# One edit of a mixture-of-experts decoder kernel: put-backs, the norm row's spread and the spatial weights moved, and the last two output slots of a mixer used token tile by token tile

## The chip, the cores and the metric

The kernel runs on one core of a Trainium2 chip. The metric is the device time of one execution in microseconds (us); the median of several executions counts. The engines are TensorE (PE in the rows; its weight loads are PEld), VectorE (DVE), ScalarE (ACT), GpSimd (POOL) and SyncE (SP), whose queue issues most DMAs.

## What is computed

Four layers on 256 tokens of width 1024, all in float32. Mixers: layers 0 and 3 a short gated convolution, layer 1 retention, layer 2 a gated MLP with spatial weights `c_w_s`.

```python
for i in range(DEPTH):                                  # 4
    mix = (conv, retention, sgu)[i % 3](x)
    x = layer_norm(ALPHA * x + mix, ln_g[i, 0], ln_b[i, 0])
    ffn = moe(x)              # 16 experts, 4 groups, top 2, router shared by the layers
    x = layer_norm(ALPHA * x + ffn, ln_g[i, 1], ln_b[i, 1])
    emb = p[i] @ ple_w_proj[i]
    x = x + sigmoid(x @ ple_w_gate[i] + ple_b_gate[i]) * emb
```

## The kernel before

**Tiling.** The tokens are two tiles (t = 0, 1) of 128. `x` holds the current rows. Each engine has one hand-written program, and they meet in semaphores. PSUM banks 0 to 3 are the sums of tile 0 (columns 0 to 511, 512 to 1023) and tile 1; banks 4 to 7 are for transposes and the rest.

**Weights.** Dense weights come in *slots* of 1 MB, loaded by SyncE into the six places of `raw`. ACT copies a slot rounded into `w_hi`, DVE makes the rest `w_lo` = `raw` - `w_hi` (`split_slot`, L1556 in the rows). A product is three matmuls (L637, L638, L639: high by high, low by high, high by low). A slot takes 12 matmuls for each tile; I call that a slot-half. `weights_used` counts slots that tile 1 has finished with; loads into their place and splits two or three slots later wait for it. Experts' weights, 96 slots a layer (8 pairs of experts, 12 slots each), are used as they are, in matmuls 64 columns wide (L1033). They are spread over all places that are free at the time: `raw`, `w_hi`, `work`, even `x` (the last one). SyncE issues all loads in one written order, each behind a wait for its place, so a load that waits holds up those behind it.

**A layer.** `first_group` and the further groups of `project_slot` are the mixer's input product; `first_group` also transposes tile 1 of `x`, the embedding `p_in` (`turn_p`) and, in layer 2, the spatial weights. Then comes the output product in rows (`rows_slot`), `last_rows` for its last three slots. The last slot of each tile ends with column half 0 and then half 1 (`half_done`, `mix_done`), and DVE starts to add it to `x` by halves (`add_rows`, L1599, with statistics L1600) and then makes the layer norm of the tile (`layer_norm`, last step L1654), tile 0 first and then tile 1. TensorE transposes tile 0 (`transpose_tile`, L648), computes part of the embedding product (L982) and the router's logits (L975), runs two filler matmuls, transposes tile 1, and finishes the logits. ACT and DVE choose the experts (`route`); TensorE computes each token's rank (L1003 to L1007), and DVE the table `pick` (`choose`, four calls).

**Experts.** For each pair p TensorE gathers (L1025), does gate and up (`wide`), transposes (`turn`), does `down`, and `put` adds the outcome y of pair p - 2 to the tiles' sums (`put_back`, L1043). For pairs 3 to 6 (`LATER`) only tile 0 is put back at once, tile 1 in the end (`put_later`). `add_x` (L1081) adds the old `x`. Behind the last `down`, the put-backs of pair 7 complete tile 0's halves (`put_half`, `ffn_done`) and then tile 1. DVE takes statistics (L1604) and makes the second layer norm. TensorE runs filler matmuls (`keep_running`, L654), transposes tile 0 and starts the gate product: `gate_slot`, whose first two slots of tile 0 are whole float32 matmuls (L788), while the next need `w_lo`. During tile 1's part DVE already builds the next layer's `x`.

**GpSimd** fetches the small rows and broadcasts them over the partitions (`load_norm` into `ln_par`, `c_ln`, `bgate`). For the next layer's first norm it waits for `x_tile_ready` = 6L + 4, when the second norm of this layer is done.

## Time and profile before

| | us |
|---|---|
| three runs | 1614.87, 1614.98, 1615.57 |
| median | 1614.98 |
| the profiled execution | 1615.02 |
| its span (first to last instruction) | 1613.2 |
| TensorE busy in the span | 1600.2 |
| DVE, ACT, GpSimd busy | 689.4, 460.4, 46.5 |
| mean granted clock of TensorE | 0.999 |
| HBM | 330 GB/s over the span; 420 to 423 in the experts |

Times in rows are us from the span's start. "Idle before" in brackets is the engine's idle time ahead of a row's first instruction and what ended it. The row of a weight load (PEld) is the best place to see TensorE wait, since matmuls' ends are modelled; some idle of 0.2 to 0.3 us ahead of a wide load is the usual pace.

### The profile page before, as it was taken

The page shows a single profiled execution, that of the slowest core. Times are in us where ns is not written, and L with a number is a line of the kernel's source. Part 1 is how long each engine was busy: PE and PEld are TensorE (multiplying, and loading weights), DVE is VectorE, ACT ScalarE, POOL GpSimd, SP SyncE. Part 2 cuts the span into 40 slices and gives each one's busy share as a digit, 9 for nine tenths or more (in the row PEclk, how much of TensorE's full clock was granted, in tenths as well). Part 3 has the DMA queues.
Part 4 walks back from the last instruction along what each step waited for, and adds up shares of the span by engine and source line. Part 5 has one row for each costly group of instructions (what it writes and reads, how often), then busy time and mean ns, then how long its engine had stood idle before and what let it go on. Part 6 is the DMA issues. An engine that isn't in the chain of part 4 may idle for free.

```text
span 1613.2 us, 17962 instructions
## 1 busy us (share of the span) xinstructions
PE 1600.2 (99%) x7576; PEld 961.3 (60%) x7584; DVE 689.4 (43%) x1023; ACT 460.4 (29%) x557; POOL 46.5 (3%) x47
## 2 busy tenths in 40 slices
PE   9999999999999999999999999999999999999998
PEld 7874433478877744433788888643434887444335
DVE  5671111294757711111956755511115767211117
ACT  5522111154433221111544433211102452211113
POOL 1000000010000000000110000000010000000000
PEclk9999999999999999999999999999999999999999
DMA  6989999946636799999557556999997388999992
GB/s 262 371 368 401 423 420 421 421 176 266 243 132 243 281 414 423 421 421 421 222 200 280 182 205 235 389 397 421 421 420 324 141 343 375 385 422 421 421 421 102
DMA packets 75146, 534.43 MB, mean 331 GB/s; under 512 B 8976, under 2 KB 9136, under 8 KB 10544
## 3 DMA queue, kind: packets, MB, share of 16 engines
q1 hardware_dynamic: 73728, 530.95, 81.2%
q0 software_dynamic: 1328, 2.21, 0.4%
q8 instruction: 65, 1.06, 0.3%
q14 instruction: 25, 0.20, 0.0%
HBM read 532.07 MB, written 1.05 MB: 330 GB/s over the span
## 4 chain that ended last, share of the span: by engine, by line
PE 90%; DVE 6%; DMA 3%; ACT 1%; issue 1%; SPq 0%; DVEq 0%; ACTq 0%
PE psum L1033 39%; PE psum L637 12%; PE psum L639 12%; PE psum L638 12%; PE psum L1025 4%; PE psum L648 3%; PE psum L1043 3%; DVE w_lo L1556 2%; PE psum L982 2%; DMA x<-in_experts 1%; DMA raw<-in_experts 1%; PE psum L975 1%; PE psum L927 1%; PE psum L872 1%; DVE x L1647 0%
## 5 line engine op out<-in xcount | busy, mean ns | idle before, releaser
L1556 DVE TENSOR_TENSOR w_lo<-raw,w_hi 128x2048 fp32r<-128x2048 f32 (+1 forms) x128 | 272.5, 2145 | 187.2 <-ACT w_hi L1248 186.7
L637 PE MATMUL psum<-w_hi,xT_hi 128*128 128x512 f32 x672 | 265.3, 395 | 3.0 <-DVE w_lo L1556 3.0
L1248 ACT ACTIVATE w_hi<-raw 128x2048 fp32r<-128x2048 f32 (+1 forms) x128 | 221.4, 1751 | 155.7 <-PE psum L639 113.1
L639 PE MATMUL psum<-w_hi,xT_lo 128*128 128x512 f32 x672 | 261.8, 390 | 0.0
L638 PE MATMUL psum<-w_lo,xT_hi 128*128 128x512 f32 x672 | 261.6, 389 | 0.0
L1248 ACT ACTIVATE work<-psum 128x512 f32<-128x512 f32 x152 | 85.8, 597 | 349.0 <-PE psum L648 247.3
L637 PEld LDWEIGHTS psum<-w_hi,xT_hi 128*128 128x128 f32 x672 | 126.2, 188 | 30.6 <-DVE w_lo L1556 4.5
L1033 PE MATMUL psum<-raw,xg 128*64 128x512 f32 x624 | 143.8, 594 | 0.0
L639 PEld LDWEIGHTS psum<-w_hi,xT_lo 128*128 128x128 f32 x672 | 126.1, 188 | 26.7
L638 PEld LDWEIGHTS psum<-w_lo,xT_hi 128*128 128x128 f32 x672 | 126.3, 188 | 25.8 <-issue 0.2
L1952 DVE TENSOR_REDUCE cg<-psum 128x1 f32<-128x256 f32 x32 | 13.6, 425 | 233.9 <-PE psum L1103 233.9
L1556 DVE TENSOR_TENSOR work_r<-psum,work_r 128x512 fp32r<-128x512 f32 x52 | 34.5, 688 | 183.7 <-ACT work_r L1248 183.7
L1248 ACT ACTIVATE xg<-psum 128x512 f32<-128x512 f32 x84 | 49.8, 597 | 203.3 <-PE psum L1025 102.1
L1033 PE MATMUL psum<-expert_work,xg 128*64 128x512 f32 x448 | 103.5, 594 | 0.0
L1033 PEld LDWEIGHTS psum<-raw,xg 128*64 128x64 f32 x624 | 43.9, 137 | 84.5 <-issue 83.9
L1033 PE MATMUL psum<-raw,work 128*64 128x512 f32 x400 | 92.9, 593 | 0.5 <-DMA raw<-in_experts 0.3
L637 PE MATMUL psum<-w_hi,work_r 128*128 128x512 f32 x224 | 89.2, 398 | 0.8 <-ACT work L1248 0.8
L639 PE MATMUL psum<-w_hi,work_r 128*128 128x512 f32 x224 | 87.6, 391 | 0.0
L638 PE MATMUL psum<-w_lo,work_r 128*128 128x512 f32 x224 | 87.5, 391 | 0.0
L1033 PE MATMUL psum<-expert_high,xg 128*64 128x512 f32 x336 | 79.5, 594 | 0.0
L1556 DVE TENSOR_TENSOR w_hi<-psum,w_hi 128x512 fp32r<-128x512 f32 x24 | 16.6, 692 | 141.7 <-ACT w_hi L1248 141.7
L1248 ACT ACTIVATE work_r<-psum 128x512 fp32r<-128x512 f32 x52 | 29.4, 600 | 159.7 <-PE psum L1033 156.2
(172 smaller groups left out, 1712.8 us busy)
## 6 DMA issues: line engine op xcount, KB each, us to landing
raw<-in_experts SPq DMA_DIRECT2D x128, 1024.0 KB, 15.9
raw<-in_slots SPq DMA_DIRECT2D x120, 1024.0 KB, 4.9
expert_work<-in_experts SPq DMA_DIRECT2D x88, 1024.0 KB, 15.4
expert_high<-in_experts SPq DMA_DIRECT2D x60, 1024.0 KB, 12.2
expert_spare<-in_experts SPq DMA_DIRECT2D x40, 1024.0 KB, 13.2
expert_bias<-in_experts SPq DMA_DIRECT2D x20, 1024.0 KB, 13.9
x<-in_experts SPq DMA_DIRECT2D x20, 1024.0 KB, 15.6
expert_norm<-in_experts SPq DMA_DIRECT2D x16, 1024.0 KB, 13.7
```

What stands on the lines that cost most here:

```text
L637: mm(out, lhs[0], rhs[0], start=start, stop=False)
L638: mm(out, lhs[0], rhs[1], start=False, stop=False)
L639: return mm(out, lhs[1], rhs[0], start=False, stop=stop)
L648: last = nc.tensor.transpose(psum[:, bank, i * P:(i + 1) * P], c, ident[:, :])
L872: last = mm(psum[:, 4 + k % 4, :], sT[:, h, (c + s) * P:(c + s + 1) * P], rv[:, s, h * DV:(h + 1) * DV], start=s == 0, stop=s == c)
L927: mm(tiles(psum[:, 4 + k % 4, 0:SVB]), sgu_wT[:, b // 2, :], sv[:, c, 3 * b:3 * b + 3, :], start=True, stop=True).then_inc(vs_in_psum, 1)
L982: last = mm(psum[:, 2 * t + c, :], pT[:, j, t * P:(t + 1) * P], whole[:, 2 * j + c, :], start=j == 0, stop=j == 1)
L1025: last = mm(psum[:, bank, j * SEQ:(j + 1) * SEQ], x_split[a][:, t, chunk], pick[:, t, Q * SEQ:(Q + 1) * SEQ], start=t + a == 0, stop=t + a ...
L1033: last = mm(psum[columns(e), bank, :], lhs(j, e), w[:, 2 * j + e, :], start=start and j == 0, stop=stop and j == 1)
L1043: last = mm(psum[:, bank0 + 2 * t + c, :], where[:, t * P:(t + 1) * P], what[i][:, c * NB:(c + 1) * NB], start=start and i == 0, stop=stop ...
L1248: return nc.scalar.activation(dst, src, func)
L1556: return tt(lo, whole, hi.bitcast(F), ALU.subtract)
```

## The change

Five things are moved; the arithmetic stays.

- GpSimd: the first `load_norm` of layers 1 to 3 is no longer made at the end of the layer before but in the layer itself, once its first six slots are used; `p_in` is fetched when the first column half of `x` is ready.
- Spatial weights (layer 2): their transposes go from before slot 3 of tile 0, bank 3, to behind `turn_p` in tile 1's part, bank 4; ACT's copy moves with them, and TensorE waits for it two slots into tile 1.
- The end of the mixer: of the last three slots the first is now used by both tiles in turn, and only the last two tile by tile.
- Put-backs: those of pair 6 for tile 0 stand behind the last `down` instead of before it; those of pair 4 for tile 1 stand with the others behind `add_x(1)`. Of the fillers, three ahead of tile 0's transposes and two behind them are dropped.
- `choose` for tile 0's first four experts stands ahead of the wait for the second rank.

```diff
--- before.py
+++ after.py
@@ -597,7 +597,7 @@
                     pool.wait_ge(x_tile_ready, 6 * L - 1)
                     pool.dma_start(sgu_w, A["c_w_s"][0].rearrange("g t s -> t g s")).then_inc(sw_loaded, 16)
                 if L:
-                    pool.wait_ge(x_tile_ready, 6 * L)
+                    pool.wait_ge(x_half_ready, 6 * L)
                     pool.dma_start(p_in, A["p"][L, 0].rearrange("(t p) d -> p t d", p=P)).then_inc(p_loaded, 16)
                 if L % 3 == 1:
                     pool.dma_start(rot, A["rotary"]).then_inc(b_loaded, 16)
@@ -607,15 +607,15 @@
                         pool.dma_start(c_ln[0:1, a, :], A[name][0].unsqueeze(0)).then_inc(gate_norm_row, 16)
                     pool.wait_ge(gate_norm_row, 32)
                     spread(c_ln[:, :, :].rearrange("p a n -> p (a n)"), c_loaded, 32)
+                if L:
+                    pool.wait_ge(weights_used, starts[L][0] + 6)
+                    load_norm(L, 0)
                 pool.wait_ge(experts_used, last_use(L, ("norm", 0)))
                 load_norm(L, 1)
                 pool.wait_ge(experts_used, last_use(L, ("bias", 0)))
                 pool.dma_start(bgate[0:1, :], A["ple_b_gate"][L].unsqueeze(0)).then_inc(bias_row, 16)
                 pool.wait_ge(bias_row, 16 * (L + 1))
                 spread(bgate[:, :], bg_loaded, 16)
-                if L + 1 < DEPTH:
-                    pool.wait_ge(x_tile_ready, 6 * L + 4)
-                    load_norm(L + 1, 0)
 
 
         @block.tensor
@@ -719,19 +719,19 @@
                 for i in range(4):
                     if i == 3:
                         transpose_tile(3 * L, 1)
-                        if L % 3 == 2:
-                            pe.wait_ge(sw_masked, 1)
-                            transpose4(3, [sgu_w[:, g, :] for g in range(SGROUPS)]).then_inc(sw_in_psum, 1)
                     project_slot(L, 0, 0, i)
                 turned_tile(3 * L, 1)
-                if L % 3 == 2:
-                    pe.wait_ge(sw_ready, 1)
                 for i in range(4):
                     if i == 2:
                         pe.wait_ge(pt_ready, L + 1)
+                        if L % 3 == 2:
+                            pe.wait_ge(sw_ready, 1)
                     project_slot(L, 0, 1, i)
                     if i == 0:
                         turn_p(L)
+                        if L % 3 == 2:
+                            pe.wait_ge(sw_masked, 1)
+                            transpose4(4, [sgu_w[:, g, :] for g in range(SGROUPS)]).then_inc(sw_in_psum, 1)
 
             def rows_slot(n, count, lhs, q, t, i, done):
 
@@ -762,8 +762,9 @@
 
             def last_rows(L, n, count, lhs):
 
+                rows_both(n, count, lhs, count - 3)
                 for t in range(T):
-                    for i in range(1, 4):
+                    for i in range(2, 4):
                         rows_slot(n, count, lhs, count // 4 - 1, t, i, mix_done)
                 transpose_tile(3 * L + 1, 0)
 
@@ -829,10 +830,10 @@
                     rows_slot(n, 4, tiled(gT), 0, t, 0, mix_done)
                     if t == 0:
                         turn_b(1)
+                rows_both(n, 4, tiled(gT), 1)
                 for t in range(T):
-                    for i in range(1, 4):
-                        if i == 2:
-                            pe.wait_ge(gT_ready[L], 3 + t)
+                    pe.wait_ge(gT_ready[L], 3 + t)
+                    for i in range(2, 4):
                         rows_slot(n, 4, tiled(gT), 0, t, i, mix_done)
                 transpose_tile(3 * L + 1, 0)
 
@@ -1156,19 +1157,17 @@
                 turn(PAIRS - 1)
                 pe.wait_ge(ident_ready, 1)
                 add_x(0)
-                put(PAIRS - 2)
                 pe.wait_ge(ht_ready, PAIRS * (L + 1))
                 down(PAIRS - 1, 0, 4)
                 pe.wait_ge(place_ready, PAIRS * (L + 1))
                 down(PAIRS - 1, 1, 7)
 
-                pe.wait_ge(y_ready, 2 * PAIRS * (L + 1) - 1)
-                put_back(place_of(PAIRS - 1), y, 0, 0, False, True).then_inc(put_half, 1)
-                put_later(LATER[1])
-                pe.wait_ge(y_ready, 2 * PAIRS * (L + 1))
-                put_back(place_of(PAIRS - 1), y, 0, 1, False, True).then_inc(ffn_done, 1)
+                for c in range(2):
+                    put_back(place_of(PAIRS - 2), outputs(L, PAIRS - 2), 0, c, False, False)
+                    pe.wait_ge(y_ready, 2 * PAIRS * (L + 1) - 1 + c)
+                    put_back(place_of(PAIRS - 1), y, 0, c, False, True).then_inc((put_half, ffn_done)[c], 1)
                 add_x(1)
-                for p in (LATER[0], *LATER[2:]):
+                for p in LATER:
                     put_later(p)
                 for c in range(2):
                     last = put_back(place_of(PAIRS - 1), y, 1, c, False, True)
@@ -1227,9 +1226,8 @@
                 experts(L)
 
                 pe.wait_ge(general_done, L + 1)
-                keep_running(3, 5)
                 transpose_tile(3 * L + 2, 0)
-                keep_running(3, 1)
+                keep_running(1, 1)
                 for i in range(4):
                     if i == 2:
                         transpose_tile(3 * L + 2, 1)
@@ -1289,6 +1287,9 @@
                     if (q, b, t) == (0, 0, 1):
                         act.wait_ge(pt_in_psum, L + 1)
                         copy(pT, psum[:, 3, :].rearrange("p (j n) -> p j n", j=2)).then_inc(pt_ready, 1)
+                        if L % 3 == 2:
+                            act.wait_ge(sw_in_psum, 1)
+                            copy(sgu_wT, quad(4)).then_inc(sw_ready, 1)
                     wait_block(act, L, b, t, proj_in_psum[L])
                     save(b, t, psum[:, 2 * t + b % 2, :]).then_inc(proj_ready[L], 1)
                     if t:
@@ -1299,9 +1300,6 @@
                 n = starts[L][0]
                 split_behind(n)
                 save_tile(3 * L, 1)
-                if L % 3 == 2:
-                    act.wait_ge(sw_in_psum, 1)
-                    copy(sgu_wT, quad(3)).then_inc(sw_ready, 1)
                 save_group(L, 0, save)
 
             def conv_mixer(L):
@@ -1900,11 +1898,12 @@
                 dve.wait_ge(rank_in_psum, 2 * L + 1)
                 link(stt(key[:, :, :], psum[:, 5, 0:T * NE].rearrange("p (t e) -> p t e", t=T), 1.0,
                          chosen[:, :, :], ALU.add, ALU.mult))
+                choose(0, slice(0, 4)).then_inc(pick_ready, 1)
                 dve.wait_ge(rank_in_psum, 2 * (L + 1))
                 step(ts(big[:, :], psum[:, 4, 0:NE], HALF + 0.5, None, ALU.is_gt))
-                for part in (slice(0, 4), slice(4, NE)):
-                    for t in range(T):
-                        choose(t, part).then_inc(pick_ready, 1)
+                choose(1, slice(0, 4)).then_inc(pick_ready, 1)
+                for t in range(T):
+                    choose(t, slice(4, NE)).then_inc(pick_ready, 1)
 
                 link(nc.vector.tensor_reduce(den[:, :], cw[:, :, :], X, ALU.add))
                 link(nc.vector.tensor_reduce(bigmax[:, :], big[:, :], X, ALU.max))
```

## Rows read from the trace of the kernel before

**Rows 1.** The page, busy us (share of the span) x instructions:
```profile
PE 1600.2 (99%) x7576; PEld 961.3 (60%) x7584; DVE 689.4 (43%) x1023; ACT 460.4 (29%) x557; POOL 46.5 (3%) x47
```
**Rows 2.** Timeline, DVE, mixer's end, layer 0: start, us, instruction [idle before]:
```profile
92.45 0.69 DVE L1599 SCALAR_TENSOR_TENSOR x<-x,psum 128x512 f32<-128x512 f32 x1 [2.70 <-PE psum L639]
...
98.41 1.42 DVE L1654 SCALAR_TENSOR_TENSOR x<-x,nrstd,ln_par 128x512 f32<-128x512 f32 x2
100.85 0.69 DVE L1599 SCALAR_TENSOR_TENSOR x<-x,psum 128x512 f32<-128x512 f32 x1 [1.03 <-PE psum L639]
```
**Rows 3.** Timeline, layer 1: DVE at tile 1, and TensorE's transposes of it:
```profile
549.25 0.69 DVE L1599 SCALAR_TENSOR_TENSOR x<-x,psum 128x512 f32<-128x512 f32 x1 [0.83 <-PE psum L639]
...
556.08 0.42 PEld L648 LDWEIGHTS psum<-const,x 128*128 128x128 f32 x4 [0.42 <-DVE x L1654]
556.74 0.42 PEld L648 LDWEIGHTS psum<-const,x 128*128 128x128 f32 x4 [0.24 <-DVE x L1654]
```
**Rows 4.** DMA share (last but one) at 149; landing: issues 149.16, 597.53, 1062.14, 1405.60:
```profile
149.00:150.00 1.00, 1.00 (x8) 0.39 (x6) 0.00 (x0) 0.85 (x2) 0.00 (x0) 1.00 0.06 25
...
DMA to landing us min/median/max: 5.2/5.2/5.2
...
DMA to landing us min/median/max: 6.0/6.0/6.0
...
DMA to landing us min/median/max: 4.7/4.7/4.7
...
DMA to landing us min/median/max: 5.5/5.5/5.5
```
**Rows 5.** Timeline, weight loads at the last expert slots, layers 0, 1, 2, 3:
```profile
314.50 0.14 PEld L1033 LDWEIGHTS psum<-x,work 128*64 128x64 f32 x2 [0.34 <-DMA x<-in_experts]
...
763.82 0.20 PEld L1033 LDWEIGHTS psum<-x,work 128*64 128x64 f32 x4 [0.94 <-DMA x<-in_experts]
...
1227.43 0.14 PEld L1033 LDWEIGHTS psum<-x,work 128*64 128x64 f32 x2 [0.29 <-DMA x<-in_experts]
...
1562.12 0.20 PEld L1033 LDWEIGHTS psum<-raw,work 128*64 128x64 f32 x4 [1.22 <-DMA raw<-in_experts]
...
1572.06 0.20 PEld L1033 LDWEIGHTS psum<-x,work 128*64 128x64 f32 x4 [0.92 <-DMA x<-in_experts]
```
**Rows 6.** Timeline, layer 0 ahead of the last `down`: TensorE, and ACT's `hT`:
```profile
308.55 0.76 PEld L1043 LDWEIGHTS psum<-xT_hi,work_r 128*128 128x128 f32 x4 [0.40 <-issue]
309.68 0.20 PEld L1033 LDWEIGHTS psum<-expert_high,work 128*64 128x64 f32 x4 [0.37 <-issue]
...
307.69 0.60 ACT L1248 ACTIVATE work<-psum 128x512 f32<-128x512 f32 x1
```
**Rows 7.** Timeline, layer 0, from the put-backs to the gate product:
```profile
322.23 0.87 PEld L1043 LDWEIGHTS psum<-work_r 128*128 128x128 f32 x4
...
323.81 1.01 PEld L648 LDWEIGHTS psum<-const,x 128*128 128x128 f32 x8
...
325.33 0.41 PEld L788 LDWEIGHTS psum<-raw,xg 128*128 128x128 f32 x2
...
324.13 1.29 DVE L1604 BATCH_NORM_STATS2 stats<-psum 128x6 f32<-128x512 f32 x2
```
**Rows 8.** Timeline, gate product, layer 0; the last row is layer 3's:
```profile
330.49 6.44 DVE L1556 TENSOR_TENSOR w_lo<-raw,w_hi 128x2048 fp32r<-128x2048 f32 x2
...
332.58 2.35 POOL L584 PARTITION_BROADCAST ln_par<-ln_par  x1 [1.33 <-DMA ln_par<-in_ln_b]
...
336.99 0.19 PEld L637 LDWEIGHTS psum<-w_hi,xT_hi 128*128 128x128 f32 x1 [1.21 <-DVE w_lo L1556]
...
1587.70 4.48 DVE L1556 TENSOR_TENSOR w_lo<-raw,w_hi 128x2048 fp32r<-128x2048 f32 x2
```
**Rows 9.** Timeline, start of layer 2, DVE and TensorE:
```profile
807.71 2.28 DVE L1556 TENSOR_TENSOR w_lo<-raw,w_hi 128x2048 fp32r<-128x2048 f32 x1
...
810.65 0.42 PEld L648 LDWEIGHTS psum<-const,emb 128*128 128x128 f32 x4 [1.06 <-DVE emb L1794]
811.04 0.19 PEld L637 LDWEIGHTS psum<-w_hi,xT_hi 128*128 128x128 f32 x1
```
**Rows 10.** Timeline, TensorE at the kernel's start:
```profile
0.99 3.59 PE L669 MATMUL psum<-ones 128*128 128x256 bf16 x16 [0.99 <-POOL ones L577]
...
6.12 2.35 PE L669 MATMUL psum<-ones 128*128 128x256 bf16 x20
```

## The prediction

> **What bounds the kernel now.** I read the busy table first: TensorE is busy for 99% of the span [rows 1]. The kernel holds some 7,500 matmuls and the change removes only eight filler matmuls (two in each of four layers). So time can move only where TensorE waits. I then went through its weight-load rows for gaps longer than the usual one, and through the chain that ended last. Each layer has four places where another resource decides.
> (a) *Between mixer and router.* The transposes of token tile 1 wait for DVE's layer norm: 0.42 and 0.24 us of idle in layer 1 [rows 3].
> (b) *Inside and at the end of the experts.* The last weight slot, which lands in `x`, is used the moment it arrives. In layers 0 and 2 TensorE is there at the same time. In layers 1 and 3 it waits: 0.94 and 0.92 us instead of the usual 0.29, and in layer 3 another 1.22 us a little earlier [rows 5].
> (c) *In the gate product.* DVE's split of a weight slot is late by 1.2 us, in layers 0, 1 and 2 but not in 3 [rows 8].
> (d) *At the start of layer 2.* TensorE waits 1.06 us for the mask of the spatial weights [rows 9].
>
> **Part 1, the row spread.** In layers 0 to 2 GpSimd fetches and broadcasts the next `ln_par` just when DVE makes the two `w_lo` that the gate product waits for. Two such subtractions take 6.44 us beside the 2.35 us broadcast, and 4.48 us in layer 3, where there is none [rows 8]. So the broadcast costs DVE 1.96 us and TensorE some 1.16 us of the 1.21 of idle (0.05 is usual between such loads). Moved to `weights_used` = first + 6, the broadcast falls into the projections. TensorE shows no wait for `w_lo` there, since slots are split two to three slots ahead of use (12 matmuls at 0.23 us for each token tile, 5.5 us a slot). I price its new place at 0. Without that cover it costs at most the same 1.96 us in each of layers 1 to 3. What is queued behind it on GpSimd (the second `load_norm`) waits for the experts anyway. The earlier fetch of `p_in` is worth 0: nobody waits for it.
>
> The Trainium skill (SBUF — State Buffer, Who interferes with whom) says that a DVE operation with two SBUF inputs contends with a GpSimd instruction that reads SBUF. By that rule the collision is moved, not removed, wherever a `w_lo` meets the broadcast again. The trace agrees on the collision; it cannot show the new one.
>
> **Part 2, put-backs and fillers.** The four put-back matmuls of pair 6 for tile 0 leave the place before `down(7)`. There they cost 309.68 - 308.55 = 1.13 us; with the fixed switch of some 0.4 us between kinds of matmul, and `hT` copied by 308.29, `down(7)` can start at 308.5, so 1.15 us earlier [rows 6]. That pays only where TensorE, not a DMA, is last (below). Behind `down(7)` the first six matmuls are as many as before, so `ffn_done` for tile 0 comes at the same distance. But four put-backs of pair 4 now stand behind it: 24 instead of 20 matmuls, 4 x 0.22 = 0.9 us more. Against that stand the removed fillers: three ahead of the transposes (0.45 us), which now start 0.46 us later, and two behind them, which lay beside ACT's copy. The first gate matmul at 325.33 waits for this copy [rows 7], so it comes 0.46 us later, too. The second tile's statistics, at 324.13 when DVE came free, wait for the later put-back: +0.37 us for DVE.
> Together with part 1: the gate product's late slot (336.99) could start at 336.99 - 1.16 + 0.46 = 336.29, and DVE has it by 336.93 - 1.96 + 0.37 = 335.34. TensorE is now last. Gain 1.16 - 0.46 = **0.70 us in each of layers 0 to 2, together -2.1**. In layer 3 there was no wait to win: **+0.46**.
>
> **Part 3, spatial weights.** Layer 2 loses the wait at 810.65. But `w_lo` for the same slot ends at 809.99 [rows 9], so slot 3 can start at 810.05 at the earliest instead of 811.04: 0.99. The four transposes (0.42 us and a switch) are paid later, behind `turn_p`, and 2.7 us of matmuls cover the ACT copy that is now waited for. **-0.5 us.**
>
> **Part 4, the choice of slots** (`choose` ahead of `big`) is the same work in another order, and TensorE has `embed` matmuls to do meanwhile: 0.
>
> **Part 5, the last output slots.** This is the largest term, and it is a loss. DVE starts on tile 0 at 92.45, when the first half is summed, and ends its norm at 98.41 + 1.42 = 99.83: 7.38 us. It then idles 1.03 us until tile 1's half comes at 100.85 [rows 2]. The two halves are three slot-halves apart (8.4 us). In the new order they are two apart, 5.6 us. So DVE comes to tile 1 late by 7.38 - 5.6 = 1.77 us in layer 0, and by 2.75 - 0.83 = 1.92 in layer 1 [rows 3]; layers 3 and 2 repeat these within 0.01. The transposes of tile 1 already wait for this norm, so the router and the first expert start **R = 1.77, 1.92, 1.92, 1.77 us** later. What the new order gives (splits of the last slots needed 2.8 us later, one slot's buffers free 5.5 us sooner) relieves nothing that waits in this trace.
>
> How much of R reaches the end of the experts? TensorE there gains back the 1.15 us of part 2. The DMA queue decides more. In the second expert pair the queue has run dry or nearly so: in layer 0 the mean share of the DMA engines is 0.06 at 149 us, and the load issued at 149.16 lands 5.2 us later. The loads at the same place in layers 1, 2 and 3 take 6.0, 4.7 and 5.5 us [rows 4]. 4.7 is the shortest there is, so the slack is 0.5, 1.3, 0 and 0.8. That issue waits for an expert slot to be used, so it moves by R. From there to the `x` slot the DMAs run without a hole. The end of the experts thus moves by R less the slack: **1.3, 0.65, 1.9, 1.0, together +4.9 us**. TensorE's own way gives less in each (R - 1.15 is at most 0.77).
>
> **Sum.** -2.1 + 0.46 - 0.5 + 4.9 = +2.8 us. The profiled execution took 1615.02 us (span 1613.2, 1.8 around it), the median of the runs is 1614.98. Forecast **1617.8 us**, with its own range of 1616.3 to 1619.4: the slack is known to about 0.3 us in each layer.
>
> **Rivals.**
> *A. The loads do not follow TensorE.* Two loads of a layer go out 5.5 us sooner, and the lag of the DMA train may be made up before the second pair. Then only R - 1.15 in layers 0 and 2 is left, 0.6 + 0.8, and nothing in 1 and 3, where TensorE waits 1.3 to 1.6 us at the end: 1.4 - 2.1 + 0.46 - 0.5 = -0.8, **1614.2 us**. Against it: the hole in the DMA share stands right at the issue that hangs on TensorE.
> *B. All of R arrives* (7.4 instead of 4.9): +5.3, **1620.3 us**. For it: in layer 0 the engines' mean share already shows a whole hole; only the slowest engine's landing leaves 0.5.
> *C. The other side: DVE is not late.* If the norm of tile 0 fitted between the two halves, R would be 0 and the relieved splits and earlier buffers would count: -2.1 + 0.46 - 0.5 = -2.1, and up to -1 us a layer where DMAs are last (1 and 3): -4, **1611.0 us**. It decides from the point where the norm takes under 5.6 us; it takes 7.38, back to back. Little speaks for it but something unseen.
> *D. The clock falls.* TensorE will be idle for about 2.2 us ahead of tile 1's transposes, in every layer; no gap of the trace is that long with the clock granted in full. At the start 16 matmuls of 256 columns took 3.59 us (the 1.2 GHz level), 20 of them 2.35 us at 2.4 GHz [rows 10], after 4.6 us of work. If each layer paid half of such 4.6 us: 4 x 2.3 = 9.2, **1627 us**. The Trainium skill (TensorE: Matmul & The Clock Gate, What's actually happening) has the clock fall after an idle window; it would give rival D for a wait long enough, and my sum for a shorter one. That the moved broadcast finds no cover (+2 a layer at most) ends at a similar place and shares this chance.
>
> **Chances.** Forecast 0.50, A 0.17, B 0.15, C 0.12, D 0.06. The range takes in A to B and most of C's side: 1612.3 to 1621.0. A measurement of this kernel can tell about 0.2%, 3.2 us, from no change. Of the forecast's own range about 4 in 10 lies above 1618.2. So slower 0.20 + 0.15 + 0.05 = 0.40, faster 0.11, the same 0.49.
>
> **What would show it.** Right: in layer 0 the second `L1599` row of tile 1 starts without idle some 2.8 us after its place, and the transposes of tile 1 wait about 2.2 us; the two `w_lo` of the gate take 4.5 us in layers 0 to 2 and TensorE's 1.2 us wait there is gone; the wait for `emb` in layer 2 is gone; the span from the router to the last `x` slot is as long as before or shorter by under 1.2 us. Wrong: a wait of the transposes as short as now (C), longer waits for `x` in layers 1 and 3 gone (A), a granted clock below full after the mixers (D), or new waits for `w_lo` in the projections.

## The result, and the profile after

The changed kernel takes 1632.04 us (median of 4 runs, 1629.44 to 1636.35) beside 1615.28 us before (1614.87 to 1615.95): ratio 1.0108, 95% interval 1.0095 to 1.0120. It is slower by 16.8 us. The forecast was 1617.8, and even the upper end of its range, 1621.0, lies 11 us too low. The profiled execution is the slowest of the four, at 1636.35 us (span 1634.5), so what follows accounts for 21.3 us between the profiled executions. The other three had a mean clock of 0.989 to 0.994 instead of 0.988. One single execution of all those below, of experiment 2's kernel, fell in a slow state (1805.90 us at a mean clock of 0.850) and stands in no ratio.

The page of the changed kernel, busy time, granted clock in 40 slices and the chain that ended last:
```profile
PE 1613.3 (99%) x7564; PEld 970.7 (59%) x7564; DVE 686.2 (42%) x1023; ACT 461.3 (28%) x557; POOL 46.1 (3%) x47
...
PEclk9989999999999999999999999899999999999999
...
PE 87%; DMA 6%; DVE 6%; issue 1%; ACT 1%; SPq 0%; DVEq 0%; ACTq 0%
```
TensorE has fewer matmuls than in [rows 1] and is busy for 13.1 us longer. That points to a slower clock, and two slices of the clock row (from 82 and from 1022 us) show an 8 in place of a 9. The windows of the changed kernel say how low it was (us; PE, PEld, DVE, ACT, POOL busy; PEclk; DMA share; GB/s):
```profile
110.00:120.20 10.20, 10.20 (x32) 6.73 (x30) 5.03 (x18) 2.34 (x4) 0.00 (x0) 0.50 0.62 256
564.00:574.20 10.20, 10.20 (x32) 6.75 (x30) 4.94 (x18) 2.34 (x4) 0.00 (x0) 0.50 0.85 357
1031.70:1041.80 10.10, 9.75 (x30) 6.94 (x31) 5.69 (x19) 2.34 (x4) 0.00 (x0) 0.50 0.69 289
1383.30:1390.00 6.70, 6.70 (x24) 5.15 (x24) 3.13 (x15) 2.17 (x4) 0.00 (x0) 0.50 0.87 359
```
0.50 is the 1.2 GHz level. Each layer has one such stretch, 10.24, 10.24, 10.24 and 6.83 us long, and each begins in the router, at the transposes of token tile 1 (in layer 2 at 1031.61, within the wait that ends at 1032.05). The kernel before had the clock in full there. What stands just ahead of it, in the changed kernel's timeline of layer 0 (start, us, instruction; TensorE's weight loads, then VectorE):
```profile
107.71 0.21 PEld L654 LDWEIGHTS psum<-const 128*128 128x128 bf16 x2
109.69 0.46 PEld L648 LDWEIGHTS psum<-const,x 128*128 128x128 f32 x4 [1.77 <-DVE x L1652]
...
111.24 3.49 PEld L976 LDWEIGHTS psum<-const,xg 128*128 128x128 f32 x16 [0.17 <-ACT xg L1246]
...
115.67 0.34 PEld L983 LDWEIGHTS psum<-raw,emb 128*128 128x128 f32 x1 [0.52 <-issue]
...
122.27 0.19 PEld L1026 LDWEIGHTS psum<-work_r 128*128 128x128 f32 x1 [0.24 <-issue]
```
```profile
95.62 0.69 DVE L1597 SCALAR_TENSOR_TENSOR x<-x,psum 128x512 f32<-128x512 f32 x1 [5.36 <-PE psum L639]
...
101.58 1.41 DVE L1652 SCALAR_TENSOR_TENSOR x<-x,nrstd,ln_par 128x512 f32<-128x512 f32 x2
102.91 0.68 DVE L1597 SCALAR_TENSOR_TENSOR x<-x,psum 128x512 f32<-128x512 f32 x1
```
VectorE begins 3.2 us later than in [rows 2], 102.91 follows 101.58 with no idle time where 1.03 us stood before, and the transposes wait 1.77 us where 0.42 stood. So VectorE is late, as the prediction's R says; 0.42 and R would have made the wait 2.2 us, but TensorE itself comes 0.62 us later to the router. Behind it the logits' 16 weight loads take 3.49 us, and the `embed` loads come 0.85 us apart: at full clock it is 1.86 us and 0.43 (below, `fill_wait`).

The rest of the changed kernel: one `w_lo` pair of the gate, the start of layer 2, the gate's transposes in layer 2, and the `x` slots of layers 0 to 3:
```profile
337.56 4.48 DVE L1554 TENSOR_TENSOR w_lo<-raw,w_hi 128x2048 fp32r<-128x2048 f32 x2
...
820.16 0.19 PEld L637 LDWEIGHTS psum<-w_hi,xT_hi 128*128 128x128 f32 x1 [0.49 <-DVE w_lo L1554]
...
1254.92 0.85 PEld L648 LDWEIGHTS psum<-const,x 128*128 128x128 f32 x8 [2.36 <-issue]
...
321.59 0.20 PEld L1034 LDWEIGHTS psum<-x,work 128*64 128x64 f32 x4 [1.33 <-DMA x<-in_experts]
...
774.90 0.20 PEld L1034 LDWEIGHTS psum<-x,work 128*64 128x64 f32 x4 [1.24 <-DMA x<-in_experts]
...
1243.41 0.20 PEld L1034 LDWEIGHTS psum<-x,work 128*64 128x64 f32 x4 [1.34 <-DMA x<-in_experts]
...
1593.26 0.20 PEld L1034 LDWEIGHTS psum<-x,work 128*64 128x64 f32 x4 [1.34 <-DMA x<-in_experts]
```
The two `w_lo` take 4.48 us instead of 6.44 [rows 8], the wait for `emb` [rows 9] has turned into 0.49 us for `w_lo`, and TensorE now waits for `x` in all four layers, where layers 0 and 2 had no such wait [rows 5]. The 2.36 us ahead of 1254.92 belong to no part of the prediction.

To add this up, cut each layer at four starts of TensorE's weight loads: the router's first logits, the first gather, the first use of the `x` slot, the gate product. The stretches between, in us, layers 0, 1, 2, 3 (the last stretch runs to the next layer's router; in layer 3 to the last load of the gate's whole float32 matmuls, L788 before and L789 after):

| kernel | router to gather | gather to `x` | `x` to gate | gate to next router |
|---|---|---|---|---|
| before | 10.94, 10.95, 10.93, 10.94 | 198.49, 199.43, 198.44, 199.62 | 10.83, 10.50, 10.88, 10.47 | 228.11, 243.74, 123.19, 6.22 |
| after | 16.58, 16.58, 16.34, 15.02 | 199.32, 198.71, 199.03, 199.80 | 10.70, 10.70, 12.85, 10.69 | 227.33, 242.45, 122.18, 6.12 |
| difference | 5.64, 5.63, 5.41, 4.08 | 0.83, -0.72, 0.59, 0.18 | -0.13, 0.20, 1.97, 0.22 | -0.78, -1.29, -1.01, -0.10 |

Sums: 20.8 + 0.9 + 2.3 - 3.2, and 0.6 up to the first router, make 21.3 us. (Example, layer 0 after: gather 122.27 less logits 105.69 is 16.58.) The router alone holds nearly all of it.

### The profile page after: what moved, and what is told of

It reads as the page before. It is cut to its first block, busy times and chain, and to the rows that moved or that the text cites. A ratio compares the mean times of both kernels' runs of the same rounds, so it can differ in the third digit from the quotient of the medians.

```text
span 1634.5 us, 17926 instructions
## 1 busy us (share of the span) xinstructions
PE 1613.3 (99%) x7564; PEld 970.7 (59%) x7564; DVE 686.2 (42%) x1023; ACT 461.3 (28%) x557; POOL 46.1 (3%) x47
## 4 chain that ended last, share of the span: by engine, by line
PE 87%; DMA 6%; DVE 6%; issue 1%; ACT 1%; SPq 0%; DVEq 0%; ACTq 0%
PE psum L1034 36%; PE psum L637 11%; PE psum L639 11%; PE psum L638 11%; DMA x<-in_experts 6%; PE psum L1026 4%; PE psum L1044 3%; PE psum L648 3%; PE psum L789 2%; PE psum L983 2%; DVE w_lo L1554 1%; PE psum L976 1%; DVE stats L1598 1%; DVE x L1645 1%; PE psum L928 1%
## 5 line engine op out<-in xcount | busy, mean ns | idle before, releaser
L1554 DVE TENSOR_TENSOR w_lo<-raw,w_hi 128x2048 fp32r<-128x2048 f32 (+1 forms) x128 | 269.1, 2119 | 189.8 <-ACT w_hi L1246 189.4
L1554 DVE TENSOR_TENSOR w_hi<-psum,w_hi 128x512 fp32r<-128x512 f32 x24 | 16.6, 692 | 141.6 <-ACT w_hi L1246 141.6
L1026 PE MATMUL psum<-work_r 128*128 128x256 f32 x512 | 75.0, 295 | 0.0
## 6 DMA issues: line engine op xcount, KB each, us to landing
expert_norm<-in_experts SPq DMA_DIRECT2D x16, 1024.0 KB, 13.1
```

Source lines behind the costliest of these rows:

```text
L1026: last = mm(psum[:, bank, j * SEQ:(j + 1) * SEQ], x_split[a][:, t, chunk], pick[:, t, Q * SEQ:(Q + 1) * SEQ], start=t + a == 0, stop=t + a ...
L1554: return tt(lo, whole, hi.bitcast(F), ALU.subtract)
```

## The experiments

Beside the experiments the kernel before gave medians of 1615.6 to 1615.7 (22 to 32 runs between 1612.9 and 1621.5, a wider spread than beside the changed kernel). All lines of diffs are against the kernel before, unless the text says otherwise.

**1. The order alone.** Only the order of the last three output slots is changed.
```diff
+                rows_both(n, count, lhs, count - 3)
                 for t in range(T):
-                    for i in range(1, 4):
+                    for i in range(2, 4):
```
(and the same in `conv_mixer`.)

> The kernel before with the new order of the last three output slots alone. Theory: DVE comes to tile 1 late by 1.8 to 1.9 us, TensorE idles 1.8 us ahead of the transposes of tile 1, its granted clock falls to the 1.2 GHz level (0.5 in the trace) for about 10 us in every layer, and router and first gather are late by some 6 us a layer: 1615 + 4 x 6 = about 1638, less a little that the end of the experts takes back (1635 to 1640). Rival, my prediction's own sum: the lateness alone, +5, about 1620, clock full. Rival, fillers: the loss comes from the put-backs and the dropped fillers; then this kernel is within 1 us of 1615.

Measured: 1632.75 us, ratio 1.0093 (1.0070 to 1.0116), clock 0.986. The window of its lowest clock in layer 0, and TensorE's matmuls ahead of it:
```profile
110.70:120.80 10.10, 10.10 (x31) 7.00 (x31) 4.61 (x17) 2.30 (x4) 0.00 (x0) 0.50 0.58 244
```
```profile
109.97 1.77 PE L648 MATMUL psum<-const,x 128*128 128x128 f32 x8 [1.28 <-DVE x L1655]
```
The order alone makes a loss as large as the whole change's; the router takes 16.6 to 16.7 us in all four layers.

**2. The change with the order undone.** The kernel after with the old loops in `last_rows` and `conv_mixer`:
```diff
-                rows_both(n, count, lhs, count - 3)
                 for t in range(T):
-                    for i in range(2, 4):
+                    for i in range(1, 4):
```


> The changed kernel with the old order of the last three output slots; everything else of the change is kept. Theory: clock full throughout, the waits of 1.2 us in the gate products and of 1.06 us at layer 2's start stay away: 1615 - 3 x 1.2 - 0.5 = about 1611 (1610 to 1613). Rival, fillers: the clock still falls and the time stays near 1630.

Measured: 1616.59 us (median of ten; 1616.18 without the one at 1805.90), ratio 1.0008 (0.9995 to 1.0022). Its window over the same stretch and the one beside the odd wait, then its timeline:
```profile
110.00:120.20 10.20, 10.20 (x53) 6.14 (x52) 7.38 (x28) 2.13 (x4) 0.00 (x0) 1.00 0.96 390
1238.00:1241.00 3.00, 1.29 (x10) 0.93 (x10) 2.93 (x8) 0.66 (x2) 0.00 (x0) 1.00 0.95 391
```
```profile
1239.65 0.85 PEld L648 LDWEIGHTS psum<-const,x 128*128 128x128 f32 x8 [2.22 <-issue]
```
The clock is full in this execution, and the router is back at 10.95 us. But the gain that I expected is not there. The stretches say where it went: gate to next router is 1.16, 1.67 and 1.24 us shorter, 4.1 in all. Against that stand 1.8 us more from `x` to gate in layer 2, which is the wait above, again in layer 2, and 3.0 us in the four stretches from gather to `x` (200.25, 199.87, 199.73, 199.18). These last scatter in every kernel of this study, between 198.4 and 200.6, also from layer to layer within one execution.

**3. The change with work in the wait.** The kernel after with ten fillers of 512 columns, two before, ahead of token tile 1's transposes:
```diff
                 logits(0)
-                keep_running(2, 7)
+                keep_running(10, 7)
                 transpose_tile(k, 1)
```


> The changed kernel, new order kept, with 10 instead of 2 filler matmuls (bf16, 512 columns, 0.21 us each) ahead of the transposes of tile 1, so that TensorE is at work while it waits for DVE. Theory: the clock stays at 2.4 GHz, only DVE's lateness of 1.8 to 1.9 us a layer is left, and of it what the load train does not hide: 1632 - 4 x 4 = about 1616 (1614 to 1618). Rival, it is not the idle stretch that brings the clock down but the light work behind it: the clock falls as before, about 1632.

Measured: 1622.19 us, ratio 1.0031 (1.0020 to 1.0043), clock 1.00. Its window and TensorE's timeline:
```profile
110.00:120.20 10.20, 9.95 (x57) 6.96 (x56) 7.95 (x26) 2.71 (x5) 0.00 (x0) 1.00 0.66 263
```
```profile
107.69 1.93 PEld L654 LDWEIGHTS psum<-const 128*128 128x128 bf16 x10
109.74 1.01 PEld L648 LDWEIGHTS psum<-const,x 128*128 128x128 f32 x8
111.24 1.86 PEld L976 LDWEIGHTS psum<-const,xg 128*128 128x128 f32 x16 [0.49 <-ACT xg L1246]
...
113.56 0.19 PEld L983 LDWEIGHTS psum<-raw,emb 128*128 128x128 f32 x1 [0.24 <-issue]
113.99 0.19 PEld L983 LDWEIGHTS psum<-raw,emb 128*128 128x128 f32 x1 [0.24 <-issue]
...
328.23 0.25 PEld L648 LDWEIGHTS psum<-const,x 128*128 128x128 f32 x2 [1.63 <-issue]
```
The transposes start when they did (109.74 against 109.69), so VectorE is just as late; but the logits behind them take 1.86 us instead of 3.49. The router takes 12.53 us in each layer. So of the router's loss 12.53 - 10.94 = 1.59 us a layer is the lateness, and 16.58 - 12.53 = 4.05, 4.05, 3.81 and 2.49 us is the clock, 14.4 in all. The remainder is larger than I expected. Of the 8.3 us between the profiled executions, 6.4 are the four 1.59, 0.6 the start of the first router, 1.9 the scatter from gather to `x`, and 2.4 stand between `x` and gate (11.93 and 11.76 in layers 0 and 1), less 3.0 up to the next routers. The row at 328.23 shows the 2.4: here TensorE stops in the middle of eight plain transposes, which wait for nothing.

**4. The row spread alone**, on GpSimd:
```diff
-                    pool.wait_ge(x_tile_ready, 6 * L)
+                    pool.wait_ge(x_half_ready, 6 * L)
...
+                if L:
+                    pool.wait_ge(weights_used, starts[L][0] + 6)
+                    load_norm(L, 0)
...
-                if L + 1 < DEPTH:
-                    pool.wait_ge(x_tile_ready, 6 * L + 4)
-                    load_norm(L + 1, 0)
```


> The kernel before with GpSimd's part alone: next norm row fetched and broadcast in the projections, p earlier. Theory: two w_lo of the gate product take 4.5 instead of 6.4 us in layers 0 to 2, TensorE's wait of 1.2 us there goes, nothing new waits: 1615 - 3 x 1.2 = 1611.5. Rival: the broadcast collides with a split in the projection and TensorE waits there instead: within 1 us of 1615.

Measured: 1613.69 us, ratio 0.9989 (0.9978 to 1.0000). Its VectorE rows at the gate of layers 0 and 2:
```profile
331.42 4.49 DVE L1556 TENSOR_TENSOR w_lo<-raw,w_hi 128x2048 fp32r<-128x2048 f32 x2
...
1243.02 4.49 DVE L1556 TENSOR_TENSOR w_lo<-raw,w_hi 128x2048 fp32r<-128x2048 f32 x2
```
From gate to next router it saves 1.08, 1.01 and 1.13 us; the term of the prediction was 1.16. The collision has moved, not gone: in the projections of layers 1 to 3 one `w_lo` each (at 393.66, 842.98 and 1305.26 us) takes 3.52, 3.70 and 3.34 us instead of 2.29. TensorE does not wait for any of the three.

**5. Put-backs alone**, the diff's order behind `down` and its fillers, nothing else.
```diff
-                put(PAIRS - 2)
...
-                keep_running(3, 5)
                 transpose_tile(3 * L + 2, 0)
-                keep_running(3, 1)
+                keep_running(1, 1)
```


> The kernel before with the new order of the put-backs behind the experts and without the fillers in front of the gate, nothing else changed. Read so far: with the order of the mixers undone, the rest of the change kept a gain of 1.2 us a layer before the next mixer (the row spread, which on its own measured 0.9989 of the time before) and still came out at 1.0008. Theory (the put-backs and the dropped fillers lose, by TensorE's instructions coming late behind the branch that ends the experts, 2.2 us in one layer or 1.5 us in two, in kernels whose code there has moved, and 0.2 us a layer else): 1617 to 1618. Rival (the loss is only scatter of the last expert loads, which landed 0.2 to 0.8 us later against the first gather in every run so far): within 1.0 of before, 1614.5 to 1616. Prediction's own term (0.7 us a layer less 0.46 in layer 3): 1613.

Measured: 1619.45 us, ratio 1.0021 (1.0012 to 1.0031). Timeline of layer 2 and the windows of its low clock:
```profile
1240.19 0.85 PEld L648 LDWEIGHTS psum<-const,x 128*128 128x128 f32 x8 [2.46 <-issue]
```
```profile
1241.50:1244.80 3.30, 3.27 (x4) 1.51 (x5) 3.06 (x9) 3.30 (x3) 0.48 (x2) 0.50 0.11 47
1371.20:1374.50 3.30, 3.30 (x5) 1.24 (x5) 3.06 (x16) 0.11 (x1) 0.00 (x0) 0.50 1.01 420
```
Part 2 is a loss by itself, 3.7 us in the median, more than expected. The odd wait stands in layer 2 for the third time, here followed by 3.4 us at 1.2 GHz, and layer 3's router lost the clock for 3.4 us as well (12.34 us instead of 10.94), though nothing ahead of it in that layer was edited.

**6. The gate's fillers dropped alone.**
```diff
-                keep_running(3, 5)
                 transpose_tile(3 * L + 2, 0)
-                keep_running(3, 1)
+                keep_running(1, 1)
```


> The kernel before with the three fillers ahead of the gate's transposes left out and one instead of three behind them; the order of the put-backs is the old one. Theory (the fillers stand beside waits and cost about 0.1 to 0.3 us a layer, and they keep no clock): 1614 to 1615, with the granted clock full. Rival 1 (the fillers are what keeps the instructions behind the branch flowing): a stall of 1.5 to 2.2 us in one or two layers shows here too, 1617 to 1618. Rival 2 (they hold the clock at the gate): stretches of 10.24 us at 1.2 GHz behind the experts, 1620 or more.

Measured: 1615.01 us, ratio 1.0000 (0.9991 to 1.0008). A window of its first router, and two of its `w_lo` pairs at the gate, layers 0 and 1:
```profile
111.30:114.60 3.30, 3.30 (x5) 1.35 (x4) 3.19 (x16) 0.00 (x0) 0.00 (x0) 0.50 1.00 422
```
```profile
332.64 4.49 DVE L1555 TENSOR_TENSOR w_lo<-raw,w_hi 128x2048 fp32r<-128x2048 f32 x2
...
780.71 6.45 DVE L1555 TENSOR_TENSOR w_lo<-raw,w_hi 128x2048 fp32r<-128x2048 f32 x2
```
Not these fillers hold the clock at the gate, and their absence costs nothing. Two things show beside that. In the first router the clock fell for 3.4 us in a stretch ahead of which this kernel is the kernel before: that stretch is near the edge without any edit. The times of the kernel before fit this: of its 83 executions beside the experiments, four with a mean clock of 0.997 took 1619.5 us on average, 22 with 0.998 took 1616.7, and the 57 others 1615.3. And who loses by the collision of `w_lo` with the broadcast is not certain either. In layer 1 the broadcast came first and the pair took 6.45 us; in layer 0 the second `w_lo` had begun at 334.84, just before the broadcast, and it was the broadcast that took longer, 4.35 us instead of 2.35:
```profile
334.94 4.35 POOL L584 PARTITION_BROADCAST ln_par<-ln_par  x1 [1.54 <-DMA ln_par<-in_ln_b]
```
The `w_lo` behind it then took 3.05 us instead of 2.29. In `wait_bare` and `order_filled` (below) layers 0 and 1 are of this second kind: pairs of 4.48 and 4.49 us, broadcasts of 4.3 to 4.4 us.

**7. The change with the order undone and the fillers kept.** Against experiment 2:
```diff
+                keep_running(3, 5)
                 transpose_tile(3 * L + 2, 0)
-                keep_running(1, 1)
+                keep_running(3, 1)
```


> The change with the mixers' order undone and the fillers kept as before: row spread, put-backs, spatial weights and the early choice stay. The kernel without the fillers gave 1616.6 beside 1615.7. If the fillers hide the late instructions behind the branch: no such stall, 1613 to 1614. If the late instructions go by where the code lies: a stall may stand at another place or none, 1613 to 1617, and whatever stalls show add up to the difference from 1613. If the put-backs lose by themselves: 1616 to 1617 without a stall behind the branch.

Measured: 1617.15 us, ratio 1.0013 (1.0004 to 1.0022). Timeline of layer 2 at the same place:
```profile
1238.38 0.33 PEld L654 LDWEIGHTS psum<-const 128*128 128x128 bf16 x3 [0.26 <-issue]
1238.83 1.01 PEld L648 LDWEIGHTS psum<-const,x 128*128 128x128 f32 x8
```
No odd wait, and it is still slower than before. From `x` to gate it takes 11.54, 11.38, 11.38, 11.38 us, against 10.46 with the old put-backs and the same fillers (`spread_alone`). With the fillers dropped it is 10.7. The kernel with the old put-backs and no fillers (`fillers_dropped`) takes 10.18, 10.17, 10.76 and 10.42. So the new order of the put-backs costs 0.9 us a layer with the fillers and 0.3 to 0.5 without, and the odd wait on top.

**8. The order alone, with work in the wait.** Against experiment 1:
```diff
-                keep_running(2, 7)
+                keep_running(10, 7)
```


> The kernel before with the new order of the last output slots alone, and ten fillers of 512 columns instead of two in front of token tile 1's transposes of the last mixer. With two fillers it gave 1632.75 (ratio 1.0093) at a clock of 0.986. Theory (the wait drops the clock, and VectorE's lateness of 1.8 to 1.9 us a layer reaches the end in full): clock 1.00 throughout and before plus 7 to 8, 1622 to 1624. The prediction's term (part of the lateness is taken up by the last loads of the experts): 1619 to 1620. Rival (the clock falls by the short pieces of work, not by the wait): still 0.986 to 0.99 and 1630 or more.

Measured: 1624.34 us, ratio 1.0055 (1.0042 to 1.0069), clock 0.999. Window of layer 0's router; the gate's fillers in layer 1:
```profile
110.00:120.20 10.20, 9.95 (x57) 6.97 (x56) 7.97 (x26) 2.69 (x5) 0.00 (x0) 1.00 0.67 267
```
```profile
778.27 0.33 PEld L654 LDWEIGHTS psum<-const 128*128 128x128 bf16 x3 [2.35 <-issue]
```
The same router, 12.53 us in each layer. Filling the wait takes 8.4 us off experiment 1. What is left, 8.6, is more than the 4.9 by which the prediction let the lateness reach the end, also when the wait of 2.35 us is taken off. This odd wait now stands in layer 1, with the old put-backs and ahead of the gate's fillers: neither the new put-backs nor the missing fillers are needed for it.

**9. The old order with less work ahead of the transposes.**
```diff
-                keep_running(2, 7)
```


> The kernel before, order and all, with the two fillers ahead of token tile 1's transposes taken out, so that TensorE is idle there for about 0.8 us instead of 0.42 (the new order made it 1.77). Nothing else changed. Theory (the clock falls by the idle time ahead of the transposes): with 0.8 us it falls in none or some of the four layers, and each layer in which it falls costs 1.4 to 4: 1615 to 1631, with stretches at 1.2 GHz that begin behind this wait and nowhere else. Rival (the fall needs the new order itself, by the lighter work around it): clock 1.00 everywhere and 1615 to 1616.

Measured: 1622.97 us, ratio 1.0038 (1.0025 to 1.0051), clock 0.99. TensorE's matmuls in layer 0 of the kernel before:
```profile
107.42 0.38 PE L654 MATMUL psum<-const 128*128 128x512 bf16 x1
107.72 1.32 PE L648 MATMUL psum<-const,x 128*128 128x128 f32 x8
```
and of `wait_bare`, with its windows:
```profile
107.87 1.32 PE L648 MATMUL psum<-const,x 128*128 128x128 f32 x8 [0.37 <-DVE x L1653]
```
```profile
104.00:109.00 5.00, 4.62 (x29) 3.28 (x27) 4.69 (x14) 2.81 (x4) 0.00 (x0) 1.00 1.00 419
109.20:115.90 6.70, 6.69 (x20) 4.92 (x21) 3.14 (x17) 1.74 (x3) 0.00 (x0) 0.50 1.01 427
559.80:566.50 6.70, 6.70 (x24) 5.03 (x23) 3.13 (x16) 2.09 (x4) 0.00 (x0) 0.50 1.01 424
1027.40:1034.10 6.70, 6.70 (x15) 3.60 (x15) 3.60 (x16) 0.34 (x2) 0.00 (x0) 0.50 1.03 427
```
This is the run that decides. With the order of before and the transposes starting as early as before (107.87 against 107.72, with a router that begins 0.15 us later), the clock falls in all four layers, for 6.83 us each (the fourth is 1372.10 to 1378.93), and the router takes 13.7 to 14.0 us instead of 10.94. Two fillers of 512 columns, 0.43 us of time, are all that is gone. The rival, that only the new order brings the fall, is out.

**10. The odd wait, moved.** Against experiment 2, in the router:
```diff
-                keep_running(2, 7)
+                keep_running(4, 7)
```


> The change with the mixers' order undone and four fillers instead of two in the route: TensorE's later instructions lie further on in its code, by two a layer, and the two more fillers run inside a wait of 0.5 us. If the wait of 2.2 us that TensorE had in layer 2 behind the branch at the end of the experts goes by where the code lies: it stands in another layer, or at another instruction, or not at all. If it goes by the order of the put-backs alone: it stays in layer 2 at 2.2 us. Time 1615 to 1618 in either case.

Measured: 1615.00 us, ratio 0.9994 (0.9982 to 1.0005). Timeline of layer 2:
```profile
1237.86 0.85 PEld L648 LDWEIGHTS psum<-const,x 128*128 128x128 f32 x8 [0.41 <-issue]
```
The put-backs are the same, and the wait of 2.22 us has shrunk to 0.41, in layer 2, with none in the others. So it does not go by the order of the put-backs alone. It may go by where the instructions lie in TensorE's code, by something that moves with them, or by the execution: there is one trace of each kernel. The medians (1616.2 there, 1615.0 here) don't settle it, since the clock differs, too: with two fillers in the router four of the nine executions in the ratio had a mean clock of 0.995 to 0.997, with four fillers all twelve had 0.999 or 1.000.

**11. Three parts kept**: row spread (as in experiment 4), spatial weights and early choice; order, put-backs and fillers as before. Beside experiment 4's lines:
```diff
-                            transpose4(3, [sgu_w[:, g, :] for g in range(SGROUPS)]).then_inc(sw_in_psum, 1)
...
+                            transpose4(4, [sgu_w[:, g, :] for g in range(SGROUPS)]).then_inc(sw_in_psum, 1)
...
+                choose(0, slice(0, 4)).then_inc(pick_ready, 1)
```


> The kernel before with the row spread, the spatial weights and the early choice; put-backs, fillers and the mixers' order as before. By the runs so far (row spread alone 1.8 less, spatial weights 0.6 in the profile, early choice nothing): 1613.0 to 1613.8, clock 1.00, no wait behind the branch. Rival (the spatial weights' gain doesn't reach the end, or it moves the code so that a wait of 1.5 to 2.2 us shows behind the branch): 1614 to 1616.

Measured: 1612.77 us, ratio 0.9984 (0.9973 to 0.9995), the fastest kernel of the study. Its `w_lo` pair at the gate, and the start of layer 2:
```profile
330.87 4.48 DVE L1556 TENSOR_TENSOR w_lo<-raw,w_hi 128x2048 fp32r<-128x2048 f32 x2
```
```profile
808.36 0.19 PEld L637 LDWEIGHTS psum<-w_hi,xT_hi 128*128 128x128 f32 x1 [0.47 <-DVE w_lo L1556]
```
Gate to next router in layer 1 is 242.15 us against 242.73 with the row spread alone: the spatial weights save 0.6 us.

**12. The same with four fillers in the router.** Against experiment 11:
```diff
-                keep_running(2, 7)
+                keep_running(4, 7)
```


> The same as parts_kept with four fillers instead of two ahead of token tile 1's transposes. The idle time there, 0.42 us, becomes none, and the transposes start 0 to 0.1 us later. If executions of the kernel before lose the clock there now and then: 0.5 to 1 less than parts_kept in the median and a narrower range of runs. If they don't: 0 to 0.5 more than parts_kept. If the later code brings a wait behind the branch: 1.5 to 2.2 more.

Measured: 1614.71 us, ratio 0.9991 (0.9981 to 1.0002). Each router takes 11.23 us instead of 10.95, together 1.1 more. The profiled execution (1619.18 us) also has this in layer 2's mixer, which the edit does not touch, followed by 3.4 us at 1.2 GHz:
```profile
1337.21 0.19 PEld L637 LDWEIGHTS psum<-w_hi,work_r 128*128 128x128 f32 x1 [2.87 <-ACT work L1248]
```
In the kernel before this wait was 0.8 us. Two more fillers buy nothing here: the median is 1.9 us above `parts_kept`.

## Why the prediction was wrong

**The step that failed is the clock, which the sum puts at nothing.** It stands in the prediction only as rival D, and there it is too small in its chance and in its price. Rival D had the right mechanism and the right place, for a chance of 0.06, and its sign (a clock below full after the mixers) came true. It said that no gap of the trace as long as 2.2 us had the clock in full, and that 16 matmuls at the start ran at 1.2 GHz [rows 10], and stopped there. The trace held the warning: ahead of those transposes the kernel had two fillers that compute nothing, and the router's other work is small. The prediction does not speak of them; in the kernel before they were what kept the clock (experiment 9). The price of 2.3 us a layer was half of a warm-up of 4.6 us at the start, and that was misread: 4.6 is when the slow matmuls ended, they took 3.59 us [rows 10], half of which is 1.8. The measured price is 4.05, 4.05, 3.81 and 2.49 us, 14.4 in all in the profiled executions (9.9 between the medians of the changed kernel and `fill_wait`), because the low stretch lasts 10.24 us in three layers and the router's work beside it takes double. The Trainium skill (TensorE: Matmul & The Clock Gate, What's actually happening) lets the clock fall after an idle window. The trace agrees in that the fall stands at the transposes' wait. But waits of 2.2 and 2.4 us behind the experts left the clock in full (1239.65 in experiment 2, 1254.92 in the changed kernel), and in `wait_bare` it fell behind 0.37 us of idle time. So idle time alone did not tell the two apart.

**The second step: how much of R arrives.** R itself was right: 1.77 to 1.92 us forecast; VectorE reaches tile 1 at 102.91 instead of 100.85 in layer 0, and measured on TensorE it is 1.59 in the router and about 0.3 ahead of it (gate to next router is 0.2 to 0.4 us longer in the changed kernel than in experiment 2, in all three layers). (Two small slips in the working: layer 1's lateness takes the halves' distance as 2.75 us where layer 0's has 2.8, and the parts of +4.9 add up to 4.8.) I let the DMA train take up 0.5, 1.3, 0 and 0.8 of it. From first gather to `x` slot the changed kernel takes 199.32, 198.71, 199.03 and 199.80 us, a mean of 199.2 where before has 199.0. The five kernels with a late router have means of 199.1 to 199.5, the nine others 199.0 to 199.8, and the two groups are 0.3 us apart (199.26 against 199.53). So little or nothing was taken up: up to 0.3 us a layer can't be told from the scatter, while the prediction had 0.65 on average. This stretch has nearly its own length, and it begins with the gather. That was rival B (1620.3, chance 0.15). Without the fall of the clock the change costs 6.5 us (`fill_wait`, median), where B had 5.3 and the forecast 2.8; some of the 6.5 is the odd wait.

**Part 1, row spread**: -1.16 a layer; measured -1.01 to -1.13 alone. Right for the pair of executions compared. But since in kernels that did not move the broadcast `w_lo` was not always the one that waited, its average worth may be less: the median fell by 2.0 us with an interval from nothing to 3.6.

**Part 2, put-backs and fillers**: gate product +0.46 late. (Where the prediction first counts the removed fillers it says eight; they are five a layer, 20 in all, and its working for this part has the five.) From `x` to gate it measured -0.13, +0.20 and +0.22 against before in layers 0, 1 and 3. The term was too large against this execution of the kernel before; against the runs with the old put-backs and no fillers the new order costs 0.3 to 0.5 us (experiment 7). What it lacked was the odd wait of some 2 us: with it part 2 costs 3.7 us as measured alone. `down(7)` did come earlier (its first load by 0.9 to 1.5 us, against the gather) and it was worth nothing, as said: `x` waits 1.2 to 1.3 us for its DMA in every layer.

**Part 3, spatial weights**: -0.5; measured -0.6. The slot waits 0.49 us for `w_lo`, as the working had it. **Part 4** was not measured by itself; the router of `parts_kept`, which has it, takes 10.95 us, as before.

**Rival C** (VectorE is not late, 1611.0) is out by the row at 102.91, which follows the norm of tile 0 without a gap, and by the wait of 1.77 us. **Rival A** (the loads do not follow, 1614.2) is out by the stretches from gather to `x`: if the loads had kept their times, these would have become shorter by R.

**The sum as it should have been**, from the runs: R in full, 4 x 1.9 = 7.6; clock 14.4; gate to next router -4.2 (parts 1 and 3, experiment 2); part 2 between `x` and gate +0.3 and the odd wait +2.0; scatter of the experts' loads +0.9; a later start of the whole kernel +0.4. That is 21.4, where the profiled executions differ by 21.3. Its terms come from these executions, so this is a booking of them and no forecast. The median, 16.8, is lower, and the other runs had a higher mean clock; by how much less it fell in each layer no trace shows.

## What stays open

Where the instructions of the odd wait are held up is not shown. The trace names nothing that TensorE waits for (in `fill_wait` it stops between two transposes of one group). It stood behind the branch that ends the experts, in layer 2 in three kernels with the same number of TensorE instructions (a fourth, `fillers_dropped`, waits 1.19 us there and takes 0.6 us longer from `x` to gate than in layer 0), in layers 0 and 1 in `fill_wait`, in layer 1 in `order_filled`, and nearly vanished when two matmuls a layer were added. Late arrival of code would fit these; no run measured it. Each kernel was profiled once, so how often the wait comes in a kernel's other executions is open, too. Nor was it separated whether in the router it is the idle time or the absence of wide matmuls that lets the clock fall: the fillers change both at once.

## What to carry to other kernels

Matmuls that compute nothing, ahead of a wait, are part of the kernel's clock: before an edit lengthens that wait, price the fall, which here was up to 4 us at each place, more than the wait itself. When tiles go through another engine in turns, halves of work of 5.6 us can't hide a 7.4 us norm, and where a DMA-bound stage starts on that result, nearly all of the lateness arrives. And a bundle of edits hides its members: three parts of this one gained 2.8 us together, and the other two cost all of it and 17 us more.

## What the runs showed of the hardware

- The low level came in stretches of 3.41, 6.83 and 10.24 us. What TensorE had done ahead of them in the router: 16-column logits, two fillers or none, the wait, 128-column transposes.
- In the same kernels, waits of 1.2 us inside the gate product [rows 8] left the clock at 2.4 GHz. Those of 2.2 to 2.5 us behind the put-backs did so in three kernels (the changed one, experiments 2 and 8), and in a fourth it fell for 3.4 us (experiment 5).
- A stop of TensorE of 1.4 to 2.5 us with no producer that the profile knows, which stands in other layers in other kernels (1.63 and 1.41 us in `fill_wait`, 2.22 in experiment 2, 2.46 in experiment 5).
- The collision of a GpSimd broadcast with VectorE's subtraction, 6.44 against 4.48 us for two [rows 8], is paid by the one that starts later: in layer 0 of `fillers_dropped` the broadcast took 4.35 us instead of 2.35, in layer 1 the pair of subtractions 6.45. The Trainium skill (SBUF — State Buffer, Who interferes with whom) has the two contend wherever they meet; the runs agree, and moved into the projections it cost one subtraction a layer 1.0 to 1.4 us and TensorE nothing (`spread_alone`).
